# A hybrid decoder block on one core: the order of the last tiles in the routing tail

## Chip, cores and metric
One of the eight cores of a Trainium2 chip runs the whole block. The metric is the device time of one execution in microseconds, as the median of several runs.

## The reference
A decoder block of 1024 tokens and 1024 features in float32: RMS norm, an input projection, an S5 state-space mixer and an mLSTM mixer side by side, an output projection with a residual, and then a mixture-of-experts layer whose routing is what matters here:

```python
logits = (t @ w_router + b_router).astype(jnp.float32)
top_vals, top_idx = lax.top_k(logits, TOP_K)        # 4 of 32 experts
gate = jax.nn.softmax(top_vals, axis=-1)
...
dest = pad_start[sorted_e] + (jnp.arange(n_assign) - start[sorted_e])
...
y_assign = ys[dest].astype(jnp.float32) * sorted_gate[:, None]
y = jax.ops.segment_sum(y_assign, sorted_tok, num_segments=n_tok)
```

Each token goes to the four experts with the largest logits; each expert is a clamped SwiGLU with biases; the results are weighted with the gates and added to the residual stream h, and a last RMS norm follows.

## The kernel before, in words
The kernel is a chain of stages, each with one program per engine: `project`, `mlstm`, `s5`, `project_out_route`, `experts`. A stage ends with a barrier of all engines, so the next one starts when the slowest engine of this one is done. Within a stage each engine works through its own list of instructions in the order in which the code writes them, and waits on semaphores.

The change is in `project_out_route`. It works on 8 tiles of 128 tokens. The mixers' output times `w_out` gives, per tile, a left and a right half of 512 features in PSUM banks; VectorE adds them to x (`add_left`, `add_right`, L1963), which gives h2. Then each tile goes through a chain over all engines:

- ScalarE sums the squares (`square_of`, L1767); VectorE adds the two halves' sums (`mean`, L1967); GpSimd raises to -1/2 (L1758); VectorE scales the rows (`norm`, L1975) into one of two buffers, which SyncE stores to DRAM as t (L1694).
- TensorE transposes the 1024 features in eight blocks into two banks (`turn`, L1843); ScalarE copies the two halves out (`turned_in`, L1775); TensorE multiplies with the router's weights, 8 products in float32 (16 matmul records) and the bias row (`choose_from`, L1856 and L1857).
- VectorE finds the four largest logits and their experts and builds a mask (`top`, L1981 to L1990); ScalarE takes the exponents (`exponent`, L1780); VectorE makes the gates (`gates`, L1994 to L1996).
- TensorE counts, with a triangle of ones and the masks of the tiles so far, each token's rank within its expert (`rank`, L1866; for the last tile also the totals, L1870). `rank(j)` waits until VectorE has read rank j-1 (L2002).
- VectorE turns ranks into addresses (`place`, L2000 to L2011), and GpSimd writes token and gate to that address of a table in DRAM with four indirect DMAs per tile (`list_places`, L1751). After all of them, SyncE loads the table as `places` (L1706).
- VectorE also spreads the gates over the 32 experts and splits them in a high and a low part (`dense`, L2015 to L2020); TensorE transposes them (`turn_gates`, L1882, for tiles 0 to 3, 4 to 6 and 7), ScalarE copies them out (`gates_in`, L1786), TensorE multiplies them with the experts' output biases (`bias`, L1891), and VectorE adds that to h2 (`add_bias`, L2028). SyncE stores h2 as h3 (L1697).
- `plan_with_bias` (L2038 to L2071) works out, from the totals, the order of the experts' passes, with `add_bias(1)` to `add_bias(7)` between its steps.

In the loop over the tiles the products of tile j run ahead of `turn(j - 1)`, `choose_from(j - 2)` and `rank(j - 3)` on TensorE, and VectorE's loop has `top(j - 2)`, `gates(j - 2)`, `place(j - 3)`, `dense(j - 3)`. What is left when the loop ends is written out by hand on each engine; that is the tail which the change reorders.

SyncE's list in the tail is: the stores of t; then for each tile j a wait for `add_bias(j)` and the store of h3 of tile j. After the store of tile 0 it waits for the last logits and loads one piece of 1 MB of the first expert's weights (L1700), waits for the stores of t and loads a second (L1703). After the store of tile 3 it waits for the lists and loads `places` (L1706). At its end it waits until `places` is in:

```python
for j in range(TT):
    sp.wait_ge(acc_read, TT + 2 * j + 2)
    sp.dma_start(h3_t[:, j, :], h2(j)).then_inc(h3_out, 16)
    if j == 0:
        sp.wait_ge(logits_ready, TT)
        sp.dma_start(early_tile(keep, 1), weights(p, 0, 1)).then_inc(keep["raw_full"][1], 16)
```

The stage `experts` follows: GpSimd gathers the first rows of t for expert 0 with an indirect DMA (L2420), TensorE transposes them (L2981), and a stream of weight pieces of 1 MB is loaded, split and multiplied for 32 experts. Its time is most of the kernel's.

Of the kernel before, what the change touches and what calls it, by code (L numbers as in the profile page):

```python
# [19 lines left out]
TT = T // P  # L20
# [1528 lines left out]
def project_out_route(nc, p, h3_dram, t_dram, table, mix, keep):  # L1549

    with ExitStack() as ctx:
# [115 lines left out]
        with nc.Block() as block:  # L1667
# [97 lines left out]
            def _(act):  # L1765
# [4 lines left out]
                def turned_in(j):  # L1770
                    for half in range(2):
                        act.wait_ge(turned, 2 * j + half + 1)
                        if j >= 2:
                            act.wait_ge(logits_ready, j - 1)
                        nc.scalar.copy(tT[:, j % 2, 4 * half:4 * half + 4, :],  # L1775
                                       psT[half][:, :].rearrange("p (k t) -> p k t", k=4)).then_inc(tT_set, 1)

                def exponent(j):
                    act.wait_ge(shifted_set, j + 1)
                    nc.scalar.activation(exps[:, j, :], shifted[:, j, :], ACT.Exp).then_inc(exp_ready, 1)  # L1780
# [25 lines left out]
                for j in range(TT):  # L1806
                    act.wait_ge(acc_read, j + 1)
                    if j:
                        act.wait_ge(squared, j)
                    square_of(j, 1, squared)  # L1810
                    if j >= 1:
                        turned_in(j - 1)
                    if j >= 2:
                        exponent(j - 2)
                exponent(TT - 2)
                gates_in(0)
                turned_in(TT - 1)
                exponent(TT - 1)
                gates_in(1)
                gates_in(2)  # L1820
# [2 lines left out]
            def _(pe):  # L1823
# [84 lines left out]
                for j in range(TT):  # L1908
                    if j < ROT:
                        pe.wait_ge(left_added, j + 1)  # L1910
                    else:
                        pe.wait_ge(acc_read, j - ROT + 1)
                    for n, k in enumerate(order):
                        if j == 0:
                            pe.wait_ge(w_lo_done, KD + n + 1)
                        mm = product(j, k, bank[j % ROT], n == 0, n == KD - 1)
                    mm.then_inc(ready, 1)
                    if j >= 1:
                        turn(j - 1)
                    if j >= 2:  # L1920
                        choose_from(j - 2)
                    if j >= 3:
                        rank(j - 3)
                choose_from(TT - 2)
                rank(TT - 3)
                turn_gates(0)
                turn(TT - 1)
                rank(TT - 2)
                bias(0)
                choose_from(TT - 1)  # L1930
                bias(1)
                rank(TT - 1)
                bias(2)
                bias(3)
                turn_gates(1)
                for j in range(4, 7):
                    bias(j)
# [4 lines left out]
            def _(v):  # L1942
# [148 lines left out]
                for j in range(TT):  # L2091
                    add_right(j)
                    mean(j)
                    norm(j)
                    if j >= 2:
                        top(j - 2)
                        gates(j - 2)
                    if j >= 3:
                        place(j - 3)
                        dense(j - 3)  # L2100
                top(TT - 2)
                gates(TT - 2)
                place(TT - 3)
                dense(TT - 3)
                add_bias(0)
                place(TT - 2)
                dense(TT - 2)
                top(TT - 1)
                gates(TT - 1)
                place(TT - 1)  # L2110
                dense(TT - 1)
                plan_with_bias()


# [940 lines left out]
```

## Time and profile before

| | us |
|---|---|
| median of 3 runs | 2232.03 (2227.58 to 2233.63) |
| the profiled execution, its own time | 2227.35 |
| its span in the profile | 2225.6 |
| share of the span with TensorE busy | 96% |
| mean granted clock of TensorE | 0.982 of 2.4 GHz |

The profile is of one execution. Its times are microseconds from the start of the span; a row of a timeline has the start, the time taken, the engine, the line of the kernel, the operation, the tiles (out<-in), the number of instructions merged in it, and in brackets how long the engine was idle before it and what is thought to have ended that. The ends of matmuls are modelled. Tiles that share memory have one name: `keep_sig_o` is here the normed rows and their transposes, `mix_qk` and `mix_v` are h2, `h` is h3 in DRAM. `SPq` rows are the issues of DMAs, not their transfer.

### The profile page before, as it was taken

The page shows a single profiled execution, that of the slowest core. Times are in us where ns is not written, and L with a number is a line of the kernel's source. Part 1 is how long each engine was busy: PE and PEld are TensorE (multiplying, and loading weights), DVE is VectorE, ACT ScalarE, POOL GpSimd, SP SyncE. Part 2 cuts the span into 40 slices and gives each one's busy share as a digit, 9 for nine tenths or more (in the row PEclk, how much of TensorE's full clock was granted, in tenths as well). Part 3 has the DMA queues.
Part 4 walks back from the last instruction along what each step waited for, and adds up shares of the span by engine and source line. Part 5 has one row for each costly group of instructions (what it writes and reads, how often), then busy time and mean ns, then how long its engine had stood idle before and what let it go on. Part 6 is the DMA issues. An engine that isn't in the chain of part 4 may idle for free.

```text
span 2225.6 us, 33282 instructions
## 1 busy us (share of the span) xinstructions
PE 2126.1 (96%) x10402; PEld 1765.4 (79%) x10403; DVE 1610.5 (72%) x1858; ACT 1211.4 (54%) x1251; POOL 587.9 (26%) x589
## 2 busy tenths in 40 slices
PE   7999987997899999999999999999999999999996
PEld 6887987686588888888888878887888888878785
DVE  4688977447855665778698675977976887677766
ACT  4423262331545554666577564757755676565655
POOL 1001031106511111334053050513511252131404
PEclk9999999997899999999999999999999999999998
DMA  7123275512976765979699795988986898777967
GB/s 186 58 86 139 86 164 190 185 57 86 351 260 215 226 223 179 338 246 373 228 359 378 233 331 180 362 284 286 364 310 224 284 369 308 244 244 282 309 238 271
DMA packets 287303, 541.66 MB, mean 243 GB/s; under 512 B 37302, under 2 KB 53798, under 8 KB 286146
## 3 DMA queue, kind: packets, MB, share of 16 engines
q1 hardware_dynamic: 262866, 495.07, 63.9%
q0 software_dynamic: 24368, 45.72, 8.2%
q8 instruction: 37, 0.61, 0.1%
q14 instruction: 32, 0.26, 0.0%
HBM read 513.61 MB, written 65.13 MB: 260 GB/s over the span
## 4 chain that ended last, share of the span: by engine, by line
PE 55%; issue 6%; DVE 6%; ACT 3%; DMA 3%; ACTq 0%; DVEq 0%; POOL 0%; SPq 0%; POOLq 0%
PE ex_ps_l L2945 7%; PE ex_ps_l L2944 7%; PE ex_ps_g L2944 6%; PE ex_ps_g L2945 6%; PE ex_ps_y L2944 5%; PE ex_ps_y L2945 5%; PE ex_ps_l L2948 4%; PE ex_ps_g L2948 4%; PE ex_ps_y L2948 3%; DVE ex_w_lo L2711 3%; PE ex_ps_t L2882 2%; ACT ex_w_hi L2579 2%; DMA ex_late<-in_w_down_dram 2%; PE ex_ps_t L2892 2%; PE ex_ps_g L2954 1%
## 5 line engine op out<-in xcount | busy, mean ns | idle before, releaser
L2711 DVE TENSOR_TENSOR ex_w_lo<-ex_late,ex_w_hi 128x2048 fp32r<-128x2048 f32 x204 | 464.2, 2291 | 222.5 <-ACT ex_w_hi L2579 154.7
L2411 POOL TENSOR_TENSOR ex_passed<-keep_ident 128x1 f32<-128x1 f32 x136 | 125.7, 924 | 1102.2 <-ACT ex_y L2622 1077.9
L2579 ACT CAST ex_w_hi<-ex_late 128x2048 fp32r<-128x2048 f32 x170 | 324.5, 1909 | 115.7 <-PE ex_ps_g L2945 60.7
L2711 DVE TENSOR_TENSOR ex_w_lo<-keep_sig_o,ex_w_hi 128x2048 fp32r<-128x2048 f32 x136 | 309.6, 2288 | 100.1 <-ACT ex_w_hi L2579 100.1
L2579 ACT CAST ex_w_hi<-keep_sig_o 128x2048 fp32r<-128x2048 f32 x134 | 255.1, 1904 | 120.6 <-PE ex_ps_l L2945 37.0
L2944 PE MATMUL ex_ps_l<-ex_w_hi,ex_x_hi 128*128 128x512 f32 x784 | 308.6, 394 | 2.0 <-DVE ex_w_lo L2711 2.0
L2944 PE MATMUL ex_ps_g<-ex_w_hi,ex_x_hi 128*128 128x512 f32 x784 | 306.5, 391 | 3.8 <-DVE ex_w_lo L2711 2.1
L2945 PE MATMUL ex_ps_l<-ex_w_lo,ex_x_hi 128*128 128x512 f32 x784 | 305.5, 390 | 0.0
L2945 PE MATMUL ex_ps_g<-ex_w_lo,ex_x_hi 128*128 128x512 f32 x784 | 305.1, 389 | 0.0
L2944 PE MATMUL ex_ps_y<-ex_w_hi,ex_h_hi 128*128 128x512 f32 x544 | 217.3, 400 | 1.2 <-DVE ex_h_lo L2747 0.9
L2945 PE MATMUL ex_ps_y<-ex_w_lo,ex_h_hi 128*128 128x512 f32 x544 | 212.1, 390 | 0.0
L2948 PE MATMUL ex_ps_l<-ex_w_hi,ex_x_lo 128*128 128x512 f32 x544 | 212.1, 390 | 0.0
L2948 PE MATMUL ex_ps_g<-ex_w_hi,ex_x_lo 128*128 128x512 f32 x544 | 211.7, 389 | 0.0
L2711 DVE TENSOR_TENSOR ex_w_lo<-keep_weights,ex_w_hi 128x2048 fp32r<-128x2048 f32 x68 | 155.6, 2289 | 27.9 <-ACT ex_w_hi L2579 24.8
L2944 PEld LDWEIGHTS ex_ps_g<-ex_w_hi,ex_x_hi 128*128 128x128 f32 x784 | 147.2, 188 | 34.4 <-issue 2.5
L2944 PEld LDWEIGHTS ex_ps_l<-ex_w_hi,ex_x_hi 128*128 128x128 f32 x784 | 147.2, 188 | 33.6 <-DVE ex_w_lo L2711 4.1
L2945 PEld LDWEIGHTS ex_ps_g<-ex_w_lo,ex_x_hi 128*128 128x128 f32 x784 | 147.2, 188 | 30.0
L2945 PEld LDWEIGHTS ex_ps_l<-ex_w_lo,ex_x_hi 128*128 128x128 f32 x784 | 147.3, 188 | 29.6
L2948 PE MATMUL ex_ps_y<-ex_w_hi,ex_h_lo 128*128 128x512 f32 x424 | 165.8, 391 | 0.0
L2579 ACT CAST ex_w_hi<-keep_weights 128x2048 fp32r<-128x2048 f32 x67 | 127.7, 1905 | 10.8 <-PE ex_ps_l L2945 7.7
L2944 PEld LDWEIGHTS ex_ps_y<-ex_w_hi,ex_h_hi 128*128 128x128 f32 x544 | 102.2, 188 | 23.2 <-DVE ex_h_lo L2747 3.7
L2948 PEld LDWEIGHTS ex_ps_l<-ex_w_hi,ex_x_lo 128*128 128x128 f32 x544 | 102.1, 188 | 21.5
(507 smaller groups left out, 4114.2 us busy)
## 6 DMA issues: line engine op xcount, KB each, us to landing
keep_sig_o<-in_w_up_dram SPq DMA_DIRECT2D x102, 1024.0 KB
ex_late<-in_w_up_dram SPq DMA_DIRECT2D x102, 1024.0 KB
ex_late<-in_w_down_dram SPq DMA_DIRECT2D x102, 1024.0 KB
keep_weights<-in_w_up_dram SPq DMA_DIRECT2D x68, 1024.0 KB
keep_sig_o<-in_w_down_dram SPq DMA_DIRECT2D x34, 1024.0 KB
st_tab<-tabs SPq DMA_DIRECT2D x8, 1408.0 KB, 12.4
keep_weights<-in_w_in_dram SPq DMA_DIRECT2D x5, 1024.0 KB, 5.5
pr_late_pieces<-in_w_in_dram SPq DMA_DIRECT2D x5, 1024.0 KB
```

What stands on the lines that cost most here:

```text
L2411: pool.tensor_tensor(passed[:, :], ident[:, 0:1], ident[:, 0:1], ALU.add).then_inc(passed_done, 1)
L2579: nc.scalar.copy(w_hi[:, j % SPLIT, :, :], raw(j)).then_inc(hi_done, 1)
L2711: v.tensor_tensor(w_lo[:, j % SPLIT, :, :], raw(j), w_hi[:, j % SPLIT, :, :].bitcast(F32), ALU.subtract).then_inc(lo_done, 1)
L2882: mm = pe.transpose(to[:, k * P:(k + 1) * P], x_rows[:, b, (4 * half + k) * P:(4 * half + k + 1) * P], ident[:, :])
L2892: mm = pe.transpose(to[:, k * P:(k + 1) * P], hidden[:, row(half, b, blocks), k * P:(k + 1) * P], ident[:, :])
L2944: pe.matmul(to[:, :], hi_in[:, b, kk, :], w_hi[:, s, k, :], start=first, stop=False)
L2945: mm = pe.matmul(to[:, :], hi_in[:, b, kk, :], w_lo[:, s, k, :], start=False, stop=last and b > 0)
L2948: mm = pe.matmul(to[:, :], lo_in[:, b, kk, :], w_hi[:, s, k, :], start=False, stop=last)
L2954: mm = pe.matmul(to[:, :], pick[:, b, :], bias_hl[:, col:col + 512], start=False, stop=True)
```

## The change
On TensorE `turn(7)` moves ahead of `choose_from(6)`, and `choose_from(7)` ahead of `bias(0)`; `bias(1)` to `bias(3)` come after `rank(7)`. On ScalarE the two copies of tile 7 move ahead of the exponent of tile 6. On VectorE the dense gates of tile 4 leave the loop and stand after `place(5)`; `place(6)` and `place(7)` come after `gates(7)`, and the dense gates of tiles 5 to 7 and `add_bias(0)` come after both. Nothing is added or left out.

```diff
@@ -1812,9 +1812,9 @@
                         turned_in(j - 1)
                     if j >= 2:
                         exponent(j - 2)
+                turned_in(TT - 1)
                 exponent(TT - 2)
                 gates_in(0)
-                turned_in(TT - 1)
                 exponent(TT - 1)
                 gates_in(1)
                 gates_in(2)
@@ -1921,17 +1921,16 @@
                         choose_from(j - 2)
                     if j >= 3:
                         rank(j - 3)
+                turn(TT - 1)
                 choose_from(TT - 2)
                 rank(TT - 3)
                 turn_gates(0)
-                turn(TT - 1)
                 rank(TT - 2)
+                choose_from(TT - 1)
                 bias(0)
-                choose_from(TT - 1)
-                bias(1)
                 rank(TT - 1)
-                bias(2)
-                bias(3)
+                for j in range(1, 4):
+                    bias(j)
                 turn_gates(1)
                 for j in range(4, 7):
                     bias(j)
@@ -2097,18 +2096,19 @@
                         gates(j - 2)
                     if j >= 3:
                         place(j - 3)
-                        dense(j - 3)
+                        if j < TT - 1:
+                            dense(j - 3)
                 top(TT - 2)
                 gates(TT - 2)
                 place(TT - 3)
-                dense(TT - 3)
-                add_bias(0)
-                place(TT - 2)
-                dense(TT - 2)
+                dense(TT - 4)
                 top(TT - 1)
                 gates(TT - 1)
+                place(TT - 2)
                 place(TT - 1)
-                dense(TT - 1)
+                for j in range(TT - 3, TT):
+                    dense(j)
+                add_bias(0)
                 plan_with_bias()
```

## Rows read from the trace of the kernel before

**Rows 1.** The page, its first part: busy time of each engine and share of the span.
```profile
PE 2126.1 (96%) x10402; PEld 1765.4 (79%) x10403; DVE 1610.5 (72%) x1858; ACT 1211.4 (54%) x1251; POOL 587.9 (26%) x589
```

**Rows 2.** Windows of core 0: length, busy (count) by engine, PEclk, DMA share, GB/s.
```profile
528.00:545.00 17.00, 11.04 (x58) 9.82 (x58) 9.82 (x48) 2.16 (x5) 11.47 (x12) 0.50 0.10 33
545.00:566.00 21.00, 12.04 (x41) 6.25 (x41) 19.20 (x72) 0.94 (x3) 7.79 (x8) 0.50 0.71 262
```

**Rows 3.** Timeline of VectorE (DVE): start, us, instruction, count, idle before and releaser.
```profile
526.58 1.28 DVE L1975 SCALAR_TENSOR_TENSOR keep_sig_o<-mix_qk,por_rstd 128x1024 f32<-128x1024 f32 x1 [0.69 <-POOL por_rstd L1758]
...
532.04 0.28 DVE L2015 TENSOR_TENSOR mix_qk<-mix_qk,por_slot 128x128 f32<-128x128 f32 x1
...
533.30 0.19 DVE L1981 MAX8 por_top_val<-por_bank 128x8 f32<-128x32 f32 x1
...
535.90 0.29 DVE L2002 TENSOR_TENSOR mix_qk<-mix_qk,por_bank 128x128 f32<-128x128 f32 x1
...
544.69 1.28 DVE L2028 TENSOR_TENSOR mix_v<-mix_v,por_bank 128x512 f32<-128x512 f32 x2 [5.89 <-DMA tabs<-keep_x_rows]
545.89 0.16 DVE L2000 TENSOR_SCALAR por_at_expert<-por_top_idxf 128x4 f32<-128x4 f32 x1
...
547.62 0.28 DVE L2015 TENSOR_TENSOR mix_qk<-mix_qk,por_slot 128x128 f32<-128x128 f32 x1
...
549.10 0.19 DVE L1981 MAX8 por_top_val<-por_bank 128x8 f32<-128x32 f32 x1
...
552.21 0.29 DVE L2002 TENSOR_TENSOR mix_qk<-mix_qk,por_bank 128x128 f32<-128x128 f32 x1 [0.50 <-PE por_bank L1870]
...
555.22 0.17 DVE L2038 COPY por_cnt_f<-por_bank 1x32 f32<-1x32 f32 x1
```

**Rows 4.** Timeline of TensorE (PE) matmuls, same columns, 528 to 552 us.
```profile
528.90 3.60 PE L1856 MATMUL por_bank<-por_w_router,keep_sig_o 128*128 128x32 f32 x16 [3.11 <-DVE por_shifted L1983]
...
534.03 1.91 PE L1843 MATMUL por_bank<-keep_ident,keep_sig_o 128*128 128x128 f32 x8
...
536.52 1.20 PE L1891 MATMUL por_bank<-por_b_split,por_gateT 96*128 96x512 f32 x2
542.40 3.62 PE L1856 MATMUL por_bank<-por_w_router,keep_sig_o 128*128 128x32 f32 x16 [4.67 <-ACT keep_sig_o L1775]
...
550.93 0.37 PE L1866 MATMUL por_bank<-por_maskb,por_onesb 128*128 128x32 bf16 x7 [3.20 <-DVE por_maskb L1990]
```

**Rows 5.** Timeline of ScalarE (ACT), the two copies of tile 7.
```profile
538.20 0.59 ACT L1775 COPY keep_sig_o<-por_bank 128x512 f32<-128x512 f32 x1 [2.97 <-issue]
541.76 0.59 ACT L1775 COPY keep_sig_o<-por_bank 128x512 f32<-128x512 f32 x1 [2.97 <-remote]
```

**Rows 6.** Timeline of SyncE's DMA issues (SPq).
```profile
546.00 0.32 SPq L1697 DMA_DIRECT2D h<-mix_v  x1
546.61 0.38 SPq L1700 DMA_DIRECT2D keep_sig_o<-in_w_up_dram  x1
...
561.28 0.32 SPq L1706 DMA_DIRECT2D keep_places<-table  x1
561.96 4.64 SPq L1697 DMA_DIRECT2D h<-mix_qk  x4
```

**Rows 7.** Timeline of GpSimd (POOL): last list issue and first gather of the experts.
```profile
557.94 0.97 POOL L1751 DMA_INDIRECT table<-por_slot,por_address  x1 [0.31 <-issue]
...
570.42 1.10 POOL L2420 DMA_INDIRECT keep_x_rows<-t,ex_gather_at  x1 [0.40 <-issue]
```

**Rows 8.** Windows again, shorter stretches; the last two numbers are DMA share and GB/s.
```profile
549.00:552.00 3.00, 1.07 (x17) 0.72 (x17) 2.43 (x13) 0.20 (x1) 2.13 (x3) 0.50 1.00 371
...
561.00:564.00 3.00, 2.78 (x6) 0.96 (x4) 3.00 (x9) 0.19 (x1) 0.00 (x0) 0.50 0.91 318
...
571.00:573.00 2.00, 2.00 (x5) 0.59 (x3) 1.80 (x1) 1.97 (x2) 1.69 (x2) 0.90 0.32 62
```

**Rows 9.** DMA issues of the window 561.2 to 561.9: KB each, us from issue to landing.
```profile
keep_places<-table SPq DMA_DIRECT2D x1, 288.0 KB, 2.9
```

## The prediction

> **What bounds the kernel now.** I read the page first, then the windows, then the timeline of each engine around the edit. On the page TensorE is busy for 96% of the span [rows 1]: most of the 2225.6 us is the expert stage. The edit lies in the routing tail, about 528 to 566 us, where TensorE has its lower clock (granted 0.50) and is busy for 11.0 of 17 us and then 12.0 of 21 [rows 2]. In the second of these windows it is VectorE that is full, 19.2 of 21 us.
>
> The timeline of VectorE names the waits [rows 3]. It has finished `dense(5)` at 538.80 and stands for 5.89 us until the two halves of `add_bias(0)` at 544.69. After that it idles once more, 0.50 us ahead of L2002 of `place(7)`, and runs almost solid from 555.22, where `plan_with_bias` begins, to the end of the stage. SyncE's last store of h3 is issued by 566.60 [rows 6], and then the stage closes. So the bound of this tail is VectorE's work plus what it stands idle, 5.89 + 0.50 = 6.39 us.
>
> Who owns the 5.89 us? The bias products stand in TensorE's records at 536.52 [rows 4], 8 us before the add that reads them. ScalarE shows the same: the eight transposes of `turn(7)` are recorded from 534.03 to 535.94, but the two copies that wait for them start at 538.20 and 541.76, each after 2.97 us of idle [rows 4, 5]. The router product of tile 7 starts right behind the second copy, at 542.40. So TensorE's signals reached their waiters up to 7 us after the recorded ends, once, in this stretch. Nothing in the profile says why.
> The Trainium skill, Perfetto Trace Analysis, Tensor Engine Instruction, says that a matmul's recorded end is an estimate and that its semaphore is pushed only after PSUM acknowledges the write; by that the copies' starts are the real times and the records are not, and the trace agrees as to direction.
>
> **The change, step by step**, all times those of the profiled execution.
> 1. `turn(7)` moves ahead of `choose_from(6)`. It needs `norm(7)`, done at 526.58 + 1.28 = 527.86 [rows 3]. TensorE idled then in any case (its next work was at 528.90 [rows 4]). Eight transposes take 1.71 us from start to the next start (eight of 0.213; they are recorded as 1.91 with the last one's tail), so `choose_from(6)` starts at 529.6 instead of 528.90: 0.7 us later. It takes 4.15 us (3.60 plus the bias row), so its logits come at 533.75.
> 2. VectorE has `place(4)` done at 532.04, and `dense(4)` no longer follows. It stands from 532.04 to 533.8: 1.7 us of new idle. Then `top(6)`, `gates(6)`, `place(5)` and one `dense` take what they took before, 533.30 to 538.80, 5.5 us: done at 539.3. The new ScalarE order puts the two copies of tile 7 ahead of `exponent(6)`; they have 529 to 530.5 to themselves, so they cost nothing. If the signals of `turn(7)` are late they stand in front of the exponent (below).
> 3. `rank(6)` needs L2002 of `place(5)`, 535.90 + 0.29 [rows 3], now 536.7. `choose_from(7)` is next behind it, starts at 537.0, and takes 4.2 us like the one at 542.40: logits at 541.2 instead of 546.6. That is the 5.4 us that the edit buys for TensorE. `bias(0)` now follows it, which costs nothing, since its reader has moved further back.
> 4. VectorE waits from 539.3 to 541.2 (1.9 us), then `top(7)` and `gates(7)` take 2.4 (549.10 to 552.21, less 0.50 idle and 0.20 for the first step of `place`), to 543.6, and `place(6)` 1.73 (545.89 to 547.62), to 545.4. `rank(7)` can start only when `place(6)` has read the bank, 0.5 us into it, at 544.1, and needs 1.28 us (550.93 to the read at 552.21), so it is ready at 545.4: no wait. `place(7)` ends at 547.1.
> 5. Three `dense` of 1.48 each (547.62 to 549.10) and `add_bias(0)` of 1.20 bring VectorE to 552.8, where it was at 555.22. By idle alone: 6.39 before, 1.7 + 1.9 = 3.6 after, 2.8 us less. I take 2.6. TensorE's bias products keep the lead that they had, since each waits for the same add as before.
> 6. The lists of places: `address` of tile 7 is set at 547.1, and POOL needs eight issues of 1.28 us for tiles 6 and 7 from 545.4, done by 555.7. Its last issue was at 557.94 [rows 7], so these go out 3 us earlier and land before SyncE asks.
> 7. SyncE's queue, which the edit does not name but moves. The store of h3 tile 0 waits for `add_bias(0)`: 546.00 becomes 552.8. Behind it in program order stand two weight pieces of 1024 KB for the experts, issued from 546.61 on [rows 6]; they become 553.3 and 553.8. Before, these 2.5 MB ran alone: the DMA share is 1.00 at 371 GB/s in 549 to 552 [rows 8]. Now the stores of tiles 1 to 3 and the load of `places` (288 KB) are issued on top of them from 554.5 to 558. The stage can't close before `places` is in. If all are served in order, 524 + 2097 + 1573 + 295 KB = 4.49 MB at 371 GB/s are 12.1 us. Counted from 553.5, some 0.7 us after the first issue (an assumption), that is about 565.6. SyncE's end then is 565.7, against 566.60 before: 0.9 us gained and not 2.6. If `places` is not held up, it lands 2.9 us after its issue, as before [rows 9], near 561, and the 2.6 us stand.
> 8. The experts' start. The stores of tiles 4 to 7 (2.1 MB, 5.6 us behind `places`) are through about 571, and the first gather, issued at 570.42 before [rows 7], goes 0.9 us earlier into that. The window 571 to 573 has a DMA share of 0.32 [rows 8], so there is room for about 1.3 us of it; I book 0.3 us against the gain.
>
> Bounds for what no row shows, the place of `places` in the queue: 2.6 us gained (overtakes all) to 1.1 lost (at the 318 GB/s of 561 to 564, where stores and this load ran together [rows 8], 14.1 us, in at 567.6). I take 371, since that row holds the very transfers that would stand in front, so 0.9.
> The Trainium skill, DMA: Bandwidth & Descriptors, Queues, rings and completion order, has each DMA engine take the descriptors of one ring in order; by that `places` waits for the weight pieces and the gain is 0.9, without it 2.6. It speaks against this change, and no row here shows such a queue, because `places` was issued into a short one.
>
> **Sum**: -0.9 + 0.3 = -0.6 us. The profiled execution took 2227.35 (span 2225.6 and 1.75 around it), so 2226.75 there; it was the fast end of the runs shown (median 2232.03, 2227.58 to 2233.63). On the median: 2231.4.
>
> **Rivals.**
> A. The places load isn't held up, and all of VectorE's gain counts: -2.6, 2229.4. For it: the queue had holes at every other place of the tail. Against it: 4.5 MB issued in 5 us. Chance 0.2.
> B. Slower: the late signals follow `turn(7)`. They began there before (3 and 5.8 us late), and now `choose_from(6)` and `exponent(6)` stand behind it. If the logits of tile 6 come at 538.4 instead of 533.75, VectorE is 4.6 us later all the way, since every step behind hangs on `top(6)`; 4.6 - 2.6 = +2.0, 2234.0. It decides from 2.6 us of lateness on. For it: three late signals in a row behind that step. Against it: the earlier turns in the loop were not late. Chance 0.15. With the lateness tied to the time and not the step (534 to 545), it would hit `choose_from(7)` by 3.3: +0.7, 2232.7; chance 0.1.
> C. The DMA backlog costs more than is gained (the bound above, 1.1 lost, and another 1 in the gather): up to +2, 2234. Chance 0.1.
> D. The change doesn't do what it says: the 5.89 us were no dependency, and VectorE waits the same sum elsewhere: 0, 2232.0. Chance 0.05.
> My forecast has 0.4.
>
> **Numbers.** A measurement of this kernel can tell about 0.3%, 6.7 us, from no change. The largest gain that the tail can give is all its idle, 6.4 us, and the largest rival costs 2; none reaches the bound alone. So within 0.3%: 0.90. Faster 0.05 (all idle gone and a lucky set), slower 0.05 (B and C together and more). The runs shown spread over 6 us, so a median moves by 2 to 3 by itself: from A less 3, 2226.5, to B plus 1.5, 2235.5.
>
> **What would show it.** In VectorE's timeline: no 5.89 us ahead of L2028; about 1.7 ahead of `top(6)` and 1.9 ahead of `top(7)`; `plan_with_bias` begins 2.6 us earlier relative to `norm(7)`. On ScalarE two copies of tile 7 near 529 to 530.5. On SyncE h3 tile 0 is issued near 552.8 and the load of `places` takes 7 us and more to land instead of 2.9. I am wrong if `choose_from(7)` starts later than 538, if the stage closes over 2 us earlier (A), or if L1775 or `top(6)` waits over 2.6 us on TensorE (B).

## The result and the profile after

| | us |
|---|---|
| median of the changed kernel, 10 runs | 2234.82 (2232.32 to 2238.95) |
| median of the kernel before, 10 runs beside it | 2229.0 (2225.8 to 2233.63) |
| ratio of the times | 1.0027, 95% interval 1.0017 to 1.0037 |
| the profiled execution, its own time | 2233.84 |
| its span | 2232.1 |

The change costs about 6 us. That has the other sign than the forecast: -0.6 us was expected, and the interval leaves no change out. That 2234.82 lies inside the range given is luck: the range was set around 2232.03, the median of three runs of the kernel before, and reached 3.5 us above it, while ten runs beside the changed kernel have 2229.0, and the change costs 5.8.

Of the eleven runs each of loads_first and vector_before below, one was far slower (5527.67 and 4001.16 us); it counts in their medians and not in their ratios.

All stages ahead of the edit ran 0.56 us later in this execution: `norm(7)` starts at 527.14, at 526.58 before [rows 3]. Times are therefore compared after taking 0.56 off, or as the distance from the start of `norm(7)`.

VectorE's timeline of the changed kernel, the answer to [rows 3] (line numbers are one smaller than before):
```profile
527.14 1.29 DVE L1974 SCALAR_TENSOR_TENSOR keep_sig_o<-mix_qk,por_rstd 128x1024 f32<-128x1024 f32 x1 [0.69 <-POOL por_rstd L1758]
...
534.30 0.20 DVE L1980 MAX8 por_top_val<-por_bank 128x8 f32<-128x32 f32 x1 [1.62 <-issue]
...
545.54 0.20 DVE L1980 MAX8 por_top_val<-por_bank 128x8 f32<-128x32 f32 x1 [5.22 <-remote]
...
555.25 1.28 DVE L2027 TENSOR_TENSOR mix_v<-mix_v,por_bank 128x512 f32<-128x512 f32 x2
556.44 0.17 DVE L2037 COPY por_cnt_f<-por_bank 1x32 f32<-1x32 f32 x1
...
566.18 1.28 DVE L2027 TENSOR_TENSOR mix_qk<-mix_qk,por_bank 128x512 f32<-128x512 f32 x2
```
The 5.89 us of idle ahead of `add_bias(0)` are gone, and 5.22 us stand ahead of `top(7)` instead. With the 1.62 ahead of `top(6)` the idle sum is 6.84, where it was 6.39. `plan_with_bias` begins at 556.44, 0.66 us later than before once the 0.56 is off. So the new order has about the idle of the old one, in other places.

TensorE's and ScalarE's timelines, the answers to [rows 4] and [rows 5]:
```profile
528.48 1.97 PE L1843 MATMUL por_bank<-keep_ident,keep_sig_o 128*128 128x128 f32 x8 [2.23 <-DVE keep_sig_o L1974]
530.25 3.46 PE L1856 MATMUL por_bank<-por_w_router,keep_sig_o 128*128 128x32 f32 x16
...
537.62 3.60 PE L1856 MATMUL por_bank<-por_w_router,keep_sig_o 128*128 128x32 f32 x16
541.15 0.63 PE L1857 MATMUL por_bank<-por_b_router,por_ones_row 1*128 1x32 f32 x2
```
```profile
529.64 0.59 ACT L1775 COPY keep_sig_o<-por_bank 128x512 f32<-128x512 f32 x1
530.49 0.59 ACT L1775 COPY keep_sig_o<-por_bank 128x512 f32<-128x512 f32 x1 [0.27 <-PE por_bank L1843]
535.11 0.20 ACT L1780 ACTIVATE por_exps<-por_shifted 128x4 f32<-128x4 f32 x1 [4.03 <-issue]
```
The turn and the copies of tile 7 are early and on time, as meant. The logits of tile 7 are recorded as done at 541.78, and `top(7)`, which VectorE was free to start from 540.3, starts at 545.54, 3.8 us after the record. The lateness did not go with the step that was moved; it stayed at its time and hit another step. (A signal is here what tells a waiting engine, through a semaphore, that an instruction is done; it is called late by how long after the recorded end the waiter starts.)

SyncE's issues, the answer to [rows 6], then GpSimd's last list issue and first gather [rows 7]:
```profile
556.55 0.32 SPq L1697 DMA_DIRECT2D h<-mix_v  x1
556.92 0.43 SPq L1700 DMA_DIRECT2D keep_sig_o<-in_w_up_dram  x1
557.46 0.87 SPq L1703 DMA_DIRECT2D keep_sig_o<-in_w_up_dram  x1
558.37 3.30 SPq L1697 DMA_DIRECT2D h<-mix_v  x3
565.66 0.32 SPq L1706 DMA_DIRECT2D keep_places<-table  x1
566.02 2.27 SPq L1697 DMA_DIRECT2D h<-mix_qk  x4
572.26 0.93 SPq L2389 DMA_DIRECT2D ex_bias_rows<-in_b_up_dram  x2
```
```profile
558.92 0.97 POOL L1751 DMA_INDIRECT table<-por_slot,por_address  x1 [0.30 <-issue]
...
575.25 1.10 POOL L2420 DMA_INDIRECT keep_x_rows<-t,ex_gather_at  x1 [0.40 <-issue]
```
The place of the DMA issue, the answer to [rows 9], and the windows that answer to [rows 2] and [rows 8]:
```profile
keep_places<-table SPq DMA_DIRECT2D x1, 288.0 KB, 5.5
```
```profile
545.00:566.00 21.00, 10.00 (x34) 4.97 (x34) 19.10 (x75) 0.94 (x3) 7.78 (x8) 0.50 0.40 127
549.00:552.00 3.00, 0.72 (x5) 0.21 (x1) 2.62 (x14) 0.00 (x0) 1.72 (x2) 0.50 0.01 0
...
561.00:564.00 3.00, 2.98 (x6) 1.42 (x6) 2.80 (x10) 0.00 (x0) 0.00 (x0) 0.50 1.05 372
...
566.00:571.00 5.00, 0.56 (x2) 0.00 (x0) 1.35 (x3) 0.00 (x0) 0.00 (x0) 0.50 1.03 419
```
Here the time went. In 549 to 552, where the two weight pieces ran at a DMA share of 1.00 before, the DMA engines now do nothing (0.01), and in 561 to 571 they are full (1.03 to 1.05 in the two windows shown). SyncE waits from 561.67 to 565.66 for the lists, 6.7 us after GpSimd's last issue at 558.92; before, it could ask 3.3 us after it (557.94 and 561.28). Then the load takes 5.5 us instead of 2.9. VectorE has been done since 567.46; the stage closes only when the places are in, at 565.66 + 5.5 = 571.16, and the experts' first issue is at 572.26 instead of 567.77: 3.9 us later with the 0.56 off.

TensorE's first transposes of gathered rows, in the kernel before and then in the changed one:
```profile
574.77 1.08 PE L2981 MATMUL ex_ps_t<-keep_ident,keep_x_rows 128*128 128x128 f32 x8 [1.50 <-DMA keep_x_rows<-t,ex_gather_at]
```
```profile
580.85 1.08 PE L2981 MATMUL ex_ps_t<-keep_ident,keep_x_rows 128*128 128x128 f32 x8 [3.03 <-DMA keep_x_rows<-t,ex_gather_at]
```
From `norm(7)` to these it was 48.19 us and is now 53.71: 5.5 us more, 3.9 at the stage's end and 1.6 up to and with the gather. From there to the end of the span it is 1650.8 and 1651.3 us: nothing is seen to be won back. The same stretch takes 1648.6 to 1653.5 us in the fourteen traces of this document, so a distance says what happened in the tail, and not to the microsecond what the whole kernel gains.

### The profile page after: what moved, and what is told of

Read it like the earlier page. It is cut to its first block, busy times and chain, and to the rows that moved or that the text cites. A ratio compares the mean times of both kernels' runs of the same rounds, so it can differ in the third digit from the quotient of the medians.

```text
span 2232.1 us, 33282 instructions
## 1 busy us (share of the span) xinstructions
PE 2130.8 (95%) x10402; PEld 1768.4 (79%) x10403; DVE 1611.1 (72%) x1858; ACT 1211.5 (54%) x1251; POOL 581.2 (26%) x589
## 4 chain that ended last, share of the span: by engine, by line
PE 57%; issue 6%; DVE 6%; ACT 3%; DMA 2%; ACTq 0%; DVEq 0%; POOL 0%; SPq 0%; POOLq 0%
PE ex_ps_l L2945 8%; PE ex_ps_l L2944 8%; PE ex_ps_g L2944 7%; PE ex_ps_g L2945 7%; PE ex_ps_y L2944 5%; PE ex_ps_y L2945 5%; PE ex_ps_l L2948 4%; PE ex_ps_g L2948 4%; PE ex_ps_y L2948 3%; DVE ex_w_lo L2711 3%; PE ex_ps_t L2882 2%; ACT ex_w_hi L2579 2%; PE ex_ps_t L2892 2%; PE ex_ps_g L2954 1%; DMA ex_late<-in_w_down_dram 1%
## 5 line engine op out<-in xcount | busy, mean ns | idle before, releaser
L2948 PEld LDWEIGHTS ex_ps_g<-ex_w_hi,ex_x_lo 128*128 128x128 f32 x544 | 102.8, 189 | 21.6
```

The lines of the kernel that those rows point to most:

```text
L2948: mm = pe.matmul(to[:, :], lo_in[:, b, kk, :], w_hi[:, s, k, :], start=False, stop=last)
```

## Experiments

Three theories were tested. **Q** (queue): the new order of VectorE makes SyncE issue the 2 MB of weights 10 us later, into the stretch where the lists, the places and the gather want the DMA engines. **P** (GpSimd): TensorE's signals reach their waiters late while GpSimd issues its indirect DMAs (the lists of places) back to back for long. **C** (clock): they are late because TensorE stands at its low clock. In the table, the distance is that from `norm(7)` to the transposes of the first gathered rows in the one profiled execution; the ratio is to the runs of the kernel before on the same chip (medians 2229.17, 2228.43 and 2228.65 of 24 or 25 runs; for the changed kernel, the ten runs above). The medians are of 8 to 11 runs, in clock of 4, and of one where that is said.

| kernel | distance | median | ratio, interval |
|---|---|---|---|
| before | 48.19 | 2229.0 | |
| changed | 53.71 | 2234.82 | 1.0027, 1.0017 to 1.0037 |
| loads_first | 48.69 | 2229.95 | 0.9999, 0.9989 to 1.001 |
| vector_before | 48.98 | 2230.05 | 1.0001, 0.9991 to 1.001 |
| before_loads_tile1 | 53.52 | 2234.15 | 1.0023, 1.0012 to 1.0034 |
| loads_behind | 55.27 | 2234.75 | 1.0033, 1.0021 to 1.0045 |
| turn_old | 53.71 | 2234.73 | 1.0028, 1.0017 to 1.0039 |
| clock | 52.51 | 2235.11 | 1.0045, 1.0029 to 1.006 |
| lists_held | 54.90 | 2237.51 (one run) | |
| after_hold5 | 52.09 | 2232.82 | 1.0027, 1.0014 to 1.0039 |
| loads_first_hold5 | 46.18 | 2226.21 | 0.9994, 0.9985 to 1.0003 |
| before_hold5 | 45.87 | 2227.49 | 0.9995, 0.9986 to 1.0004 |
| before_hold4 | 47.99 | 2226.46 (one run) | |
| before_hold5_copies | 45.31 | 2225.01 | 0.9982, 0.9972 to 0.9993 |

### What the late loads cost

**loads_first**: the changed kernel with the two pieces ahead of the stores of h3.
```diff
+                sp.wait_ge(logits_ready, TT)
+                sp.dma_start(early_tile(keep, 1), weights(p, 0, 1)).then_inc(keep["raw_full"][1], 16)
+                for b in range(2):
+                    sp.wait_ge(normed_out[b], 16 * TT // 2)
+                sp.dma_start(early_tile(keep, 2), weights(p, 0, 2)).then_inc(keep["raw_full"][2], 16)
                 for j in range(TT):
                     sp.wait_ge(acc_read, TT + 2 * j + 2)
                     sp.dma_start(h3_t[:, j, :], h2(j)).then_inc(h3_out, 16)
-                    if j == 0:
...
```


> The changed kernel, but SyncE issues the two weight pieces for the experts (1 MB each) before the store of h3 tile 0 instead of behind it. Theory Q (the queue): in the changed kernel the small writes of the last two tiles' lists and the load of places stand behind 2 MB of weights issued at 556.9 to 558.3, so places is asked for only at 565.7 and is in at 571.1. With the pieces issued at 545.6 instead, places is asked for near 562 and is in near 565, the stage closes on VectorE's end (567.5) and the experts start near 569.0 instead of 572.3; with the gather back at 4.3 us the kernel gains 3 to 5 us: 2230 to 2231.5. Theory V (VectorE's moved waits alone set the loss): the time stays at 2234.8 within 1.

SyncE's issues in it:
```profile
545.12 0.38 SPq L1696 DMA_DIRECT2D keep_sig_o<-in_w_up_dram  x1
...
556.14 5.13 SPq L1702 DMA_DIRECT2D h<-mix_v  x4
561.31 0.43 SPq L1705 DMA_DIRECT2D keep_places<-table  x1
562.76 4.64 SPq L1702 DMA_DIRECT2D h<-mix_qk  x4
568.58 0.80 SPq L2388 DMA_DIRECT2D ex_bias_rows<-in_b_up_dram  x2
```
The pieces go out at 545.12, the places are asked for 4.35 us earlier than in the changed kernel, and the stage closes 3.7 us earlier. The median is 2229.95, 4.9 below the changed kernel's. The order of TensorE, ScalarE, VectorE and GpSimd was left as changed, so that order as such costs nothing that can be measured (0.9989 to 1.001), and gains nothing.

**vector_before**: the changed kernel with VectorE's list of before; TensorE and ScalarE as changed.
```diff
...
-                dense(TT - 4)
+                dense(TT - 3)
+                add_bias(0)
+                place(TT - 2)
+                dense(TT - 2)
                 top(TT - 1)
                 gates(TT - 1)
-                place(TT - 2)
                 place(TT - 1)
-                for j in range(TT - 3, TT):
-                    dense(j)
-                add_bias(0)
+                dense(TT - 1)
```


> The changed kernel with VectorE's order of before (dense gates of every tile directly after its place, add_bias(0) ahead of place(6)); TensorE and ScalarE keep the new order. Theory Q: add_bias(0) waits for bias(0) until about 545.5 (late signals included), the store of h3 tile 0 and the two weight pieces go out near 547, the lists and places meet a short queue, and plan_with_bias begins near 555.9: as before, 2229 to 2230.5. If instead the new TensorE order is what costs, it stays at 2234 or more.

It has 2230.05. VectorE waits for TensorE's late signal where it did before:
```profile
544.68 1.28 DVE L2027 TENSOR_TENSOR mix_v<-mix_v,por_bank 128x512 f32<-128x512 f32 x2 [5.06 <-DMA tabs<-keep_x_rows]
```
So TensorE's and ScalarE's parts are not the cost. What costs is that `add_bias(0)` moved on VectorE, because a store waits for it and the loads stand behind the store.

**before_loads_tile1**: the counterpart on the kernel before. Every engine keeps its order; one number in SyncE's list changes.
```diff
-                    if j == 0:
+                    if j == 1:
                         sp.wait_ge(logits_ready, TT)
```


> The kernel before, with one edit: the two early weight pieces are issued behind the store of h3 tile 1 (near 557) instead of tile 0 (546.6). TensorE, ScalarE, VectorE and GpSimd keep the order of before. Queue theory: this alone makes the kernel before slow like the changed one: the lists' last writes land 6 to 7 us after their issue, SyncE asks for the places near 564 to 566 instead of 561.3, the experts start 3 to 4.5 us later than 567.8, and the median is 2232 to 2234 beside 2229 for before. Rival (the new order of the engines is the cost): no change, within 1 us of before.

```profile
557.38 0.43 SPq L1700 DMA_DIRECT2D keep_sig_o<-in_w_up_dram  x1
...
558.82 2.06 SPq L1697 DMA_DIRECT2D h<-mix_v  x2
564.36 0.32 SPq L1706 DMA_DIRECT2D keep_places<-table  x1
```
This edit alone gives 2234.15 (1.0023, where the change has 1.0027): the whole loss is there, within the intervals, without any of the change. The lists' last writes let SyncE go 6.0 us after GpSimd's last issue (558.35), and the places take 6.0 us. Together with loads_first this settles Q: taking the late loads out of the change removes the loss, putting them into the kernel before makes it.

**loads_behind**: the changed kernel with the pieces behind the load of the places.
```diff
+                    if j == PLACES_AT:
+                        sp.wait_ge(listed, 16 * TT * K4)
+                        sp.dma_start(keep["places"][:, 0:E * COLS, :], table.rearrange("(p c) w -> p c w", p=P)).then_inc(places_in, 16)
-                    if j == 0:
                         sp.wait_ge(logits_ready, TT)
...
-                    if j == PLACES_AT:
-                        sp.wait_ge(listed, 16 * TT * K4)
...
```


> The changed kernel, with the two early weight pieces issued behind the load of the places instead of behind the store of h3 tile 0. The question is whether it is the place of the 2 MB among the transfers that costs, and not that they are loaded early in some other stretch. Queue theory (the small writes of the lists and the load of the places stand behind the weight pieces): the lists have landed about 3 us after GpSimd's last issue, so SyncE asks for the places near 562 instead of 565.7, they are in by about 565, the stage closes on VectorE's end near 567.5 and the experts start near 569 instead of 572.3; the median is 2229.5 to 2232, unless the pieces now collide with the first gather and give some of it back. Rival (VectorE's later end alone sets the experts' start, the queue is no cost): the experts start near 572 again and the median stays at 2234.8.

```profile
560.49 0.43 SPq L1700 DMA_DIRECT2D keep_places<-table  x1
560.97 0.79 SPq L1702 DMA_DIRECT2D keep_sig_o<-in_w_up_dram  x1
...
567.77 0.93 SPq L2388 DMA_DIRECT2D ex_bias_rows<-in_b_up_dram  x2
```
```profile
581.25 1.97 PE L2980 MATMUL ex_ps_t<-keep_ident,keep_x_rows 128*128 128x128 f32 x8 [8.31 <-DMA keep_x_rows<-t,ex_gather_at]
```
The expected median (2229.5 to 2232) was missed, at 2234.75. The steps ahead of it came in: the lists landed within 2.8 us, the places in 3.6, and the experts' first issue is at 567.77, where 569 or so was expected. But now the gather stands behind the 2 MB: issued at 571.11, its rows reach TensorE at 581.25, 10.1 us later, where it took 4.35 before and 5.6 in the changed kernel. The expectation named that as an exception and did not price it. The loss moves from the places to the gather and stays as large. Of the three places tried for these 2 MB, only the one where nobody else needs the DMA engines is free; in the changed kernel that is 545 to 556, where their share is 0.00 to 0.02.

### Why signals are late

**turn_old**: the changed kernel with `turn(7)` and its copies where they were.
```diff
-                turn(TT - 1)
                 choose_from(TT - 2)
                 rank(TT - 3)
                 turn_gates(0)
+                turn(TT - 1)
...
```


> The changed kernel with turn(7) and its two copies back in their old place behind turn_gates(0). If the moved turn is worth nothing, choose_from(7) still starts right behind rank(6) near 537.5 and the time is that of the changed kernel, 2234 to 2236. If signals of TensorE come late behind turn(7) as in the kernel before (copies at 538.2 and 541.8), choose_from(7) starts near 542.4 and all of VectorE's tail is 4 to 5 us later: 2238 to 2240.

ScalarE's two copies in it:
```profile
536.56 0.59 ACT L1775 COPY keep_sig_o<-por_bank 128x512 f32<-128x512 f32 x1 [1.23 <-PE por_bank L1843]
540.12 0.59 ACT L1775 COPY keep_sig_o<-por_bank 128x512 f32<-128x512 f32 x1 [2.97 <-remote]
```
and VectorE's `top(7)`:
```profile
545.25 0.20 DVE L1980 MAX8 por_top_val<-por_bank 128x8 f32<-128x32 f32 x1 [5.98 <-PE por_bank L1857]
```
The second copy is late again (its transposes are recorded until 536.41), the router product starts at 540.76 instead of 537.62, and `top(7)` comes at 545.25, no later than in the changed kernel; 2234.73 against 2234.82. Moving the turn gained 3.1 us on TensorE and nothing for the one who waits for its result. The two kernels get to 545 by different ways. Here the product is late and its signal is not: it is recorded until 544.94, and `top(7)` starts 0.3 us after that. In the changed kernel the product is early and its signal late.

**clock**: 34 extra products on TensorE, ahead of `turn(7)` and of `rank(6)`, raise its granted clock (0.51 and 0.50 in these two windows in the changed kernel); nothing that is stored changes.
```diff
+                pe.wait_ge(acc_read, 6)
+                keep_clock(pe, bank[2], ident, 18)
                 turn(TT - 1)
...
+                keep_clock(pe, bank[2], ident, 16)
                 rank(TT - 2)
```


> The changed kernel with 18 extra products of 128 columns into a free bank ahead of turn(7) and 16 ahead of rank(6), to fill TensorE's idle time there. Theory C (the lower clock makes the signals late): with the granted clock at full the top(7) waits no longer than the recorded product, and VectorE's tail is 4 to 6 us earlier: 2230 to 2232 or less. Theory P: the products are up to twice as fast if the clock holds, but the signals of rank(6) and choose_from(7) are still 3 to 4 us late; 2232 to 2235.

Its windows (with the granted clock as the third number from the end), and ScalarE's copy of the transposed gates:
```profile
528.00:538.00 10.00, 9.96 (x93) 9.69 (x91) 7.25 (x32) 2.01 (x6) 7.97 (x8) 1.00 0.15 53
538.00:545.00 7.00, 5.27 (x33) 4.54 (x33) 2.75 (x12) 0.58 (x1) 4.12 (x5) 0.82 0.01 1
```
```profile
541.04 0.58 ACT L1786 CAST por_gateT<-por_bank 96x512 fp32r<-96x512 f32 x1 [4.74 <-DMA rhos<-pr_rho]
```
The gates' transposes are recorded from 534.66 to 535.28, at the full clock (1.00, that is 2.4 GHz), and the copy that waits for them starts 5.8 us later. The extra products stand right behind these transposes and go on until 541.69, so this run alone doesn't clear them of a part in that. `place(5)` too waits, until 539.66, for a rank recorded as done at 534.82. So the low clock is not needed for a late signal, and the next run shows that it is not enough for one. `top(7)` comes on time (545.28, its product being recorded until 545.24), against the expectation by P; GpSimd's run of issues had a gap here, from 539.58 to 541.55. The kernel is no faster for its clock: 1.0045 (1.0029 to 1.006).

**lists_held**: GpSimd issues nothing between `norm(7)` and the logits of tile 7; 20 of the lists' 32 issues come after.
```diff
+                    if j == TT - 1:
+                        pool.wait_ge(logits_ready, TT)
                     if j >= 4:
                         list_places(j - 4)
```


> The changed kernel, but GpSimd holds the lists of tiles 3 to 7 back until the logits of tile 7 are there, so no indirect DMA is issued between 523 and 542. Theory P (GpSimd's back-to-back indirect DMAs delay TensorE's signals): top(7) starts within 0.3 us of the recorded end of choose_from(7), near 541.8, not 545.5. Theory C (the lower clock or the mix of small matmuls does it): top(7) still starts 3 to 4 us late. The 20 issues of 1.28 us then run to about 568, so the whole kernel is 2 to 6 us slower, 2236 to 2240, by either.

```profile
542.05 0.20 DVE L1982 MAX8 por_top_val<-por_bank 128x8 f32<-128x32 f32 x1 [1.94 <-PE por_bank L1859]
...
567.70 0.18 DVE L2072 SCALAR_TENSOR_TENSOR keep_plan<-mix_qk 1x32 int32<-1x32 f32 x1 [1.96 <-DMA tabs<-keep_x_rows]
```
`top(7)` starts at 542.05, 0.03 us after the recorded end of its product (542.02), and the profile names TensorE as its releaser. TensorE's granted clock is 0.50 there, so theory C is refuted. The whole is slow (2237.51, one run), since the lists then end at 567.6, and VectorE meets late signals in that run of 20.

One of them is not TensorE's. Ahead of L2072 the code waits only for VectorE's own earlier steps (`steps_done`). The last of them is recorded as done at 563.12 and `add_bias(6)` behind it at 565.74, yet L2072 starts at 567.70, 0.1 us after GpSimd's last issue ends (567.56). So theory P has the releaser too narrow: VectorE's own signal came 4.6 us late as well (one wait, in one trace).

**after_hold5** and **before_hold5**: the lists of tiles 5 to 7 are held until the logits of tile 7, in the changed kernel and in the one before. **before_hold4** holds those of tiles 4 to 7, **before_hold5_copies** those of 5 to 7 only until the last copy of tile 7.
```diff
                 for j in range(TT - 4, TT):
+                    if j == TT - 3:
+                        pool.wait_ge(logits_ready, TT)
                     list_places(j)
```


> The changed kernel, but GpSimd waits for the logits of tile 7 before it issues the lists of tiles 5 to 7, so the run of back-to-back indirect DMAs ends near 538 instead of 543.9. Theory P (a long run of them delays TensorE's signals): top(7) starts near 541.8 instead of 545.5 and plan_with_bias near 552.7; SyncE's queue is still loaded behind add_bias(0), so the experts start only 3 to 4 us earlier than in the changed kernel, near 569: 2230 to 2232. If the delay has set in before 538 all the same, top(7) stays at 545 and the lists of tile 5 come later: 2235 to 2237.

> The kernel before with the same hold and nothing else. Theory P: the copies of tile 7 start behind their transposes, near 535.2 and 536.1 instead of 538.2 and 541.8, add_bias(0) near 538.9 instead of 544.7, and VectorE's tail is up to 5 us shorter, if the run of indirect DMAs up to 537.9 has not set the delay in already: 2224 to 2226. If it has (the delay was seen from 534.3 on here), the copies stay late and the time is 2229 to 2231.

> The kernel before, with the lists of tiles 4 to 7 held off until the logits of tile 7, to see how the delay follows the length of the run of indirect writes. GpSimd theory: the first run now ends with tile 3, near 532 to 533, before the transposes of tile 7 are recorded (534 to 536), so the two copies of tile 7 come within 1 us of the records, near 535.2 and 536.1, against 538.2 and 541.8 before; add_bias(0) follows near 537.2; the lists end near 562 to 563, so the places and the whole gain little: 2228 to 2232. Rival (the delay is bound to the time or to ScalarE's queue): the copies stay at 538 and 541.

> The kernel before, with the lists of tiles 5 to 7 held off only until the last copy of tile 7's transposes on ScalarE is done, and not until its logits. GpSimd theory (TensorE's signals are late while GpSimd issues its indirect writes back to back for long, and are let go soon after it stops): the first run of lists ends near 536.5 as with the other hold, the copies come near 537.2 and 538.0, and the second run starts 4 us sooner than there; choose_from(7) is then in the second run's first 4 us. If only a long run delays signals, top(7) is near 542.4 again and the lists end 4 us sooner: 2225 to 2228, experts at 563 or before. If any indirect write delays them, top(7) is at 545 or later and the gain is gone: 2229.

GpSimd's last issue of its first run in the kernel before, in before_hold5 and in before_hold5_copies:
```profile
541.86 0.97 POOL L1751 DMA_INDIRECT table<-por_slot,por_address  x1 [0.30 <-issue]
```
```profile
535.57 0.97 POOL L1751 DMA_INDIRECT table<-por_slot,por_address  x1 [0.30 <-issue]
```
```profile
538.30 0.97 POOL L1751 DMA_INDIRECT table<-por_slot,por_address  x1 [0.30 <-issue]
```
ScalarE's copies of tile 7 in before_hold5, in before_hold4 and in before_hold5_copies, to be read against [rows 5], where each has 2.97 us of idle:
```profile
537.24 0.58 ACT L1777 COPY keep_sig_o<-por_bank 128x512 f32<-128x512 f32 x1 [3.03 <-remote]
538.03 0.58 ACT L1777 COPY keep_sig_o<-por_bank 128x512 f32<-128x512 f32 x1 [0.20 <-remote]
```
```profile
535.72 0.59 ACT L1777 COPY keep_sig_o<-por_bank 128x512 f32<-128x512 f32 x1 [0.27 <-PE por_bank L1845]
536.57 0.59 ACT L1777 COPY keep_sig_o<-por_bank 128x512 f32<-128x512 f32 x1 [0.27 <-PE por_bank L1845]
```
```profile
539.24 0.58 ACT L1777 COPY keep_sig_o<-por_bank 128x512 f32<-128x512 f32 x1 [2.28 <-remote]
540.73 0.58 ACT L1777 COPY keep_sig_o<-por_bank 128x512 f32<-128x512 f32 x1 [0.90 <-remote]
```
The lateness follows GpSimd's run. With the run cut after tile 3 (ended by 533.2, ahead of the transposes recorded at 534.62) the copies come with their records. With it cut after tile 4 the last issue ends at 536.54, and the two copies come 0.7 and 1.5 us after that. In before_hold5_copies, where all the stages ahead ran 2.7 us later than in before_hold5, the last issue of the first run ends at 539.27, and the copies come at 539.24 and 540.73. In the kernel before the run goes on to 542.8, and the copies come at 538.20 and 541.76, within it, and `add_bias(0)` 1.9 us behind it. In after_hold5 `top(7)` is on time at 541.96, but in the second run of lists `place(7)` waits 1.31 us for a rank that is recorded as done:
```profile
547.91 0.29 DVE L2003 TENSOR_TENSOR mix_qk<-mix_qk,por_bank 128x128 f32<-128x128 f32 x1 [1.31 <-remote]
```
So P holds in the main: take the run away from a stretch, and the signals there are on time; the step, the time and the clock don't do it. How late a signal is within a run the runs don't settle. The same wait of `place(7)` is 3.12 us in before_hold5_copies and 2.99 in before_hold4, and in loads_first_hold5, with nearly the same issues as after_hold5 (the second run starts at 542.26 and at 542.20), there is none. Nor does any run show what in the chip ties the signals to GpSimd's indirect DMAs, or whether it is their issue or their writes.

The times came in less well than the signals. before_hold5 (2227.49) lies between the two ranges that were expected, as its copies are late by a part. after_hold5 (2232.82) is above its 2230 to 2232, and its load of the places takes 7.6 us. before_hold4, one run, has 2226.46, below its 2228 to 2232.

What it is worth: before_hold5 pulls the distance in by 2.3 us, but its ratio does not clear 1. after_hold5 has `top(7)` on time and stays at 1.0027, the ratio of the changed kernel; its pieces still go out at 555.52. With the pieces first as well,

**loads_first_hold5**: both edits, loads_first and after_hold5, on the changed kernel.

> The same hold, with the two weight pieces issued before the store of h3 tile 0 as in the earlier run. Theories P and Q together: top(7) near 541.8, last list issued near 557, places in near 563.5, the stage closes on VectorE's end near 563.7 and the experts start near 565.3, against 568.6 without the hold: 2226 to 2227.5, about 2.5 us under the kernel before. If only Q holds: 2230 as without the hold.

2226.21, as expected, and a distance of 46.18: the changed order with both of its costs taken away is about 2 us better than before by the distance, and by the runs 0.9994 with an interval that takes in 1. The best is before_hold5_copies: VectorE's work in the old order, the second run of lists started 3.5 us sooner after `norm(7)` than with the other hold, a distance of 45.31 and 2225.01 us, 0.9982 (0.9972 to 0.9993). It is the only one here whose interval lies under 1, and it has one wait on GpSimd more than the kernel before. Not all of its expectation came in: the experts start at 566.54, which is 566.54 - 528.14 = 38.40 us after `norm(7)` where before_hold5 has about the same (563.43 - 525.45 = 37.98), and 563 or before had been expected. `top(7)` is on time at 545.26, but the wait of 3.12 us ahead of `place(7)` takes what that gave. So its lead over before_hold5, 2.5 us in the medians, is not shown to lie in the tail.

## Why the prediction was wrong, step by step

**Reading of before.** That VectorE's work plus its idle bounds the tail of the kernel before, and that TensorE's signals are late in this stretch, was right. That the lateness goes with GpSimd's run of indirect DMAs was not seen; the run itself stood in [rows 2], where GpSimd has 12 instructions and is busy for 11.47 of 17 us. In the changed kernel another wait bounds the tail: the places.

**Steps 1 and 2** held. With the 0.56 off, `turn(7)` starts at 527.9 (527.86 forecast), the router product of tile 6 at 529.7 (529.6), `top(6)` at 533.7 after 1.62 us of idle (533.8 and 1.7).

**Steps 3 to 5** failed at one sentence of step 3, "logits at 541.2". The product ran from 537.62, 537.1 on the clock of before (537.0 forecast), but its signal came 3.8 us after its recorded end. The step took the recorded end for the time at which VectorE sees it, in the very stretch for which the opening had shown that the two differ by up to 7 us. Of VectorE's 2.6 us nothing was left: `plan_with_bias` begins at 555.9 on that clock, not at 552.8, and the store of h3 tile 0 behind `add_bias(0)` at 556.0 instead of 552.8.

**Step 6** failed: the lists did not land "before SyncE asks". They landed 6.7 us after the last issue, and SyncE stood 4.0 us for them.

**Step 7** had the right mechanism in part, with the wrong start. Its term was 12.1 us of backlog from 0.7 us after the first issue, 552.8. The first issue was at 556.0 on that clock. Put in, this gives 556.7 + 12.1 = 568.8, and the places were in at 571.16 - 0.56 = 570.6. So of the 5.0 us by which it missed (565.6), 3.2 come from the start, that is from step 4, and 1.8 are the term's own error; its other end, 14.1 us at the rate of [rows 8], would have given 570.8. That this sum comes near is partly luck, since the way there was another: the load of the places was not put behind the pieces by 558, as the step has it, but at 565.66, after the wait for the lists, and then took 5.5 us, not the 7 and more that were named as a sign. The Trainium skill, DMA: Bandwidth & Descriptors, Queues, rings and completion order, cited at that step, has each DMA engine take the descriptors of one ring in order; the trace agrees in direction, with 5.5 us instead of 2.9 behind the pieces. But the lists' writes, which the profile has on another queue than SyncE's loads, were held up as well (6.7 us instead of 3.3), so the order of one ring is not all of it.

**Step 8** was mis-sized: 0.3 us booked, 1.6 measured, 1.25 of it between the gather's issue and its rows (5.60 instead of 4.35).

**The sum**: forecast -0.9 + 0.3 = -0.6; measured +3.9 + 1.6 = +5.5, and +5.8 in the medians. So the steps that failed are step 3, which took a recorded end for a signal (3.8 us), and step 6, which had the lists land before SyncE asks (it stood 4.0 us for them); the queue of step 7 started 3.2 us late by the first of these.

**The rivals.** B's second form, the lateness tied to the time and hitting `choose_from(7)` by 3.3 us, is what happened on VectorE: 3.8 us there, and its end 0.66 us later where +0.7 was given. It was priced as if that were all. C had the queue, at up to +2. Each was priced with the other's part as forecast: B left the queue out, C took it that VectorE gains its 2.6 us. Both hit, and they do more together than apart: a late `add_bias(0)` also starts the backlog late, closer to the places. D, with the least chance of all, had it that VectorE waits the same sum elsewhere; so it did, 6.84 us against 6.39, but D's price of 0 left the queue out too. A, the places not held up, is refuted by 5.5 us against 2.9. Of the signs named for being wrong none came (`choose_from(7)` after 538, the stage closed early, `top(6)` or L1775 late); the one that did, on `top(7)`, stood only in rival B.

The chance for slower by over 0.3% was 0.05; the ratio's 0.27% lies just under that bound. The prediction held that less than 0.3% can't be told from no change; with ten runs of each kernel 0.27% could (1.0017 to 1.0037).

## What to carry to other kernels

When a step is moved, look in the program order of every DMA queue for what stands behind it, and price those transfers in the stretch where they will now run, together with every small transfer there that somebody waits for. A bulk load ahead of a stage's end belongs where the DMA engines are empty, and should not hang on an edit of another engine's order. And where a profile shows that signals come later than the recorded ends, no step in that stretch may be costed by recorded ends: find first what they are late with. Here, moving the turn ahead brought the product 3.1 us forward and its reader nothing.

## What the runs showed of the hardware

- While GpSimd issued indirect DMAs back to back (one each 1.28 us, runs of eight to twenty), signals reached their waiters late: TensorE's at ScalarE and VectorE up to 7.0 us after the recorded end (`add_bias(0)` before: 537.72 and 544.69), 5.8 in clock, and one of VectorE's own 4.6 us (lists_held). Some came through within the run (the copies before), others 0.1 to 1.9 us behind its end. With the run ended before the transposes, the wait was 0.27 us (before_hold4). It happened at a granted clock of 0.50 and of 1.00. Not every signal in a run was late: `top(6)` in the changed kernel, 7 us into it, was on time.
- 2 MB of loads on SyncE's queue, issued shortly before, held up the small indirect writes of GpSimd's: 5.7 to 7.0 us from the last issue until SyncE asked for the places, against 2.1 to 3.4 in the kernels whose loads went out early or behind the places. The load of the places took 5.5 to 7.6 us instead of 2.9 to 3.6, and a gather of one tile, with the 2 MB just ahead of it, 10.1 us against 4.35.
- A later entry into the expert stage was not made up for in the 1650 us behind it: from the first gathered rows to the end of the span it is 1650.8 us before and 1651.3 after, and 1648.6 to 1653.5 in all the traces.
